# Prompt attention reorganised: three-pass scores on half the array's rows, one transpose bank, TensorE order item by item

## The reference

```python
s = jnp.einsum('bqhmd,bkhmd->bhmqk', qs, ks).astype(F32) * (DIFF_DH ** -0.5)
s = s + bias[None, :, None]
s = jnp.where(rel >= 0, s, jnp.finfo(F32).min)
p = jax.nn.softmax(s, axis=-1)
a = p[:, :, 0] - lam * p[:, :, 1]
return jnp.einsum('bhqk,bkhd->bqhd', a, v.astype(F32))
```

## Time and profile before

| | |
|---|---|
| median of 3 runs | 3955.66 us (3954.72 to 3956.73) |
| the profiled execution | 3956.0 us |
| its span, first to last instruction | 3954.2 us |
| TensorE busy over the span | 92% |
| VectorE, ScalarE, GpSimd busy | 51%, 33%, 8% |
| prompt attention: first DMA to last output tile | 2194.2 to 3076.5 us |

### The profile page before, as it was taken

The page is one execution under the profiler, slowest core; times in us unless marked ns, Lnnn a source line. Parts: engine busy times, 40 slices in busy tenths (PEclk is TensorE's granted clock), DMA queues, the critical chain, the costliest instruction groups (busy, mean ns, idle before and its releaser), DMA issues. The chain is left out here.

```text
span 3954.2 us, 55321 instructions
## 1 busy us (share of the span) xinstructions
PE 3629.8 (92%) x19279; PEld 2987.5 (76%) x19279; DVE 2020.6 (51%) x4394; ACT 1323.2 (33%) x2186; POOL 319.5 (8%) x258
## 2 busy tenths in 40 slices
PE   3999997996999999999999688888898799969999
PEld 3988985774888888888888577777777767558887
DVE  1112111555732642743733588889888222156785
ACT  1112111331221322322322366666666211123332
POOL 0002002111100300200200000000000000022220
PEclk9999997998999999999999899999999899989999
DMA  4323332335334434445443622222210545254541
GB/s 111 98 90 120 102 96 80 112 112 196 115 128 133 165 123 159 160 129 166 147 136 122 134 66 66 55 53 55 66 34 12 205 176 206 106 185 165 170 159 71
DMA packets 364126, 473.00 MB, mean 120 GB/s; under 512 B 157877, under 2 KB 219094, under 8 KB 363878
## 3 DMA queue, kind: packets, MB, share of 16 engines
q1 hardware_dynamic: 363878, 469.77, 37.8%
HBM read 365.20 MB, written 104.47 MB: 119 GB/s over the span
## 5 line engine op out<-in xcount | busy, mean ns | idle before, releaser
L438 PE MATMUL mid_ps_m<-mid_w_hi,mid_x_hi 128*128 128x512 f32 x1632 | 641.0, 393 | 0.5 <-DVE mid_x_lo L594 0.5
L439 PE MATMUL mid_ps_m<-mid_w_lo,mid_x_hi 128*128 128x512 f32 x1632 | 635.8, 390 | 0.0
L440 PE MATMUL mid_ps_m<-mid_w_hi,mid_x_lo 128*128 128x512 f32 x1632 | 635.7, 390 | 0.0
L606 DVE TENSOR_TENSOR mid_w_lo<-mid_stage,mid_w_hi 128x1024 fp32r<-128x1024 f32 x192 | 239.1, 1246 | 234.8 <-ACT mid_w_hi L524 233.4
L438 PE MATMUL in_ps_m<-in_w_hi,in_x_hi 128*128 128x512 f32 (+2 forms) x952 | 344.9, 362 | 12.6 <-DVE in_x_lo L594 12.6
L440 PEld LDWEIGHTS mid_ps_m<-mid_w_hi,mid_x_lo 128*128 128x128 f32 x1632 | 306.7, 188 | 64.3
L438 PEld LDWEIGHTS mid_ps_m<-mid_w_hi,mid_x_hi 128*128 128x128 f32 x1632 | 306.8, 188 | 63.5 <-DVE mid_x_lo L594 1.7
L439 PEld LDWEIGHTS mid_ps_m<-mid_w_lo,mid_x_hi 128*128 128x128 f32 x1632 | 306.9, 188 | 61.4
L440 PE MATMUL in_ps_m<-in_w_hi,in_x_lo 128*128 128x512 f32 (+2 forms) x952 | 343.4, 361 | 0.0
L439 PE MATMUL in_ps_m<-in_w_lo,in_x_hi 128*128 128x512 f32 (+2 forms) x952 | 343.4, 361 | 0.0
L1502 PE MATMUL att_ps_o<-att_v,att_a_t 128*128 128x128 f32 x2176 | 291.8, 282 | 47.0 <-ACT att_a_t L1563 46.1
(11 more groups left out here) (278 smaller groups left out, 5622.0 us busy)
## 6 DMA issues: line engine op xcount, KB each, us to landing
mid_stage<-in_diff_w_in SPq DMA_DIRECT2D x128, 512.0 KB, 3.7
smp_k_pg<-in_cache_k SPq DMA_DIRECT2D x64, 512.0 KB, 5.1
smp_v_pg<-in_cache_v SPq DMA_DIRECT2D x64, 512.0 KB
in_stage<-in_gla_w_in SPq DMA_DIRECT2D x32, 512.0 KB, 4.0
mid_stage<-in_gla_w_out SPq DMA_DIRECT2D x32, 512.0 KB, 5.5
mid_stage<-in_ple_w_gate SPq DMA_DIRECT2D x32, 512.0 KB, 3.5
att_k_nat<-out_k SPq DMA_DIRECT2D x128, 128.0 KB, 2.6
att_q_nat<-diff_q SPq DMA_DIRECT2D x128, 128.0 KB, 2.8
```

The costliest lines, as they stand in the source:

```text
L438: nc.tensor.matmul(dst, x_hi[u][:, k, :], w_hi[r][:, i, 0:W], start=(k == 0), stop=False)
L439: nc.tensor.matmul(dst, x_hi[u][:, k, :], w_lo[r][:, i, 0:W], start=False, stop=False)
L440: mm = nc.tensor.matmul(dst, x_lo[u][:, k, :], w_hi[r][:, i, 0:W], start=False, stop=(k == KD - 1))
L606: nc.vector.tensor_tensor(lo, stage[n % STAGES][:, :, 0:W], hi.bitcast(F32), ALU.subtract).then_inc(s["w_lo_done"], 1)
```

## The change

All 128 items are written out, and each step is made anew. (Lines of the changed kernel are cited as order prints them.)

- Prep: keys and queries come in whole (two DMAs per 512 tokens in place of eight), 8 preps per head. ScalarE copies the transposed bank to `raw`, and GpSimd splits it into `hi` and `lo`.
- Scores: three passes (hi*hi, hi*lo, lo*hi) per m, on the 64 rows of that m, the two m in turn, into two of three slots of 1024 columns. Of a part (up to 1024 keys) all passes are waited for together, and the wait ahead of a part asks for both of its slots.
- Take: one VectorE instruction per part and m with the bias laid out over all keys; one reduce gives the negative maximum. Reciprocal and weight move to GpSimd (three small instructions), the scaled output tile from ScalarE to VectorE.
- Transposes of preps and of `a` share a single bank `ps_a`.
- Queues run at other distances: scores 4 items ahead of the products, take 3, exps 2.

```diff
-        ps_s = [ps(f"ps_s{i}") for i in range(RING)]
-        ps_k = ps("ps_k")
-        ps_a = [ps(f"ps_a{i}") for i in range(2)]
+    LEAD, TAKE, EXP = 4, 3, 2
+    S_BUFS, SLOTS, OUTS = 4, 3, 4
...
+        ps_s = [ps(f"ps_s{i}", WIDE) for i in range(SLOTS)]
+        ps_a = ps("ps_a")
...
+                def scores(n):
...
+                        x = 2 * (first_part[n] + c)
...
+                        if x + 2 > SLOTS:
+                            pe.wait_ge(s["taken"], after(x + 2 - SLOTS))
+                        for a0 in range(first, last, BANK):
+                            a1 = min(a0 + BANK, last)
+                            for step, (left, right) in enumerate(((hi, hi), (hi, lo), (lo, hi))):
+                                for m in range(2):
+                                    rows = slice(m * D_DH, (m + 1) * D_DH)
+                                    mm = nc.tensor.matmul(ps_s[(x + m) % SLOTS][:, a0 - first:a1 - first],
+                                                          left[u][1][rows, i * P:(i + 1) * P],
+                                                          right[u][0][rows, a0:a1], start=(step == 0),
+                                                          stop=(step == 2))
+                            if a1 == last:
+                                mm.then_inc(s["ready"], 1)
...
+                def values(n):
+                    for g in range(turns(n) + 1):
+                        if g < turns(n):
+                            turn(n, g)
+                            yield
+                        if g >= 1:
+                            meet(n, g - 1)
+                            yield
+
+                for n in range(FIRST, N):
+                    for key in preps_at(n):
+                        prep(*key)
+                    for _ in scores(n + LEAD) if 0 <= n + LEAD < N else ():
+                        pass
+                    for _ in values(n) if n >= 0 else ():
+                        pass
...
+                for n in range(FIRST, N):
+                    ahead = 0 <= n + EXP < N
+                    if ahead:
+                        exps(n + EXP, 0)
+                    for key in preps_at(n):
+                        evict(*key)
+                    middle = (turns(n) + 1) // 2 if n >= 0 else 0
+                    copies(n, 0, middle)
+                    if ahead:
+                        exps(n + EXP, 1)
+                    copies(n, middle, turns(n) if n >= 0 else 0)
...
+                for n in range(-TAKE, N + 1):
+                    if n + TAKE < N:
+                        take(n + TAKE)
+                    if 0 <= n < N:
+                        combine(n)
+                    if 1 <= n:
+                        output(n - 1)
```

More of the change, by code:

```diff
@@ L1320, in attention, with at, keys, parts @@
     T = PROMPT_TILES
+    N = D_HEADS * T
     NEAR = 2 * P
[L1322 to L1331, removed]
+    WIDE = 2 * BANK
+    LEAD, TAKE, EXP = 4, 3, 2
+    S_BUFS, SLOTS, OUTS = 4, 3, 4
+    def at(n):
+        return divmod(n, T)
+    def keys(n):
+        return (n % T + 1) * P
+    def parts(n):
+        return [(a, min(a + WIDE, keys(n))) for a in range(0, keys(n), WIDE)]
+    first_part = [sum(len(parts(m)) for m in range(n)) for n in range(N + 1)]
+    def turns(n):
+        return -(-(n % T + 1) // 4)
+    first_turn = [sum(turns(m) for m in range(n)) for n in range(N + 1)]
+    FIRST = -6
+    PREPS = 8
+    def preps_at(n):
+        here = [(0, n - FIRST)] if 0 <= n - FIRST < PREPS else []
+        if 0 <= n < N - T and n % 2 == 0:
+            here.append((n // T + 1, n % T // 2))
+        return here
+    order = [key for n in range(FIRST, N) for key in preps_at(n)]
+    prep_no = {key: m for m, key in enumerate(order)}
+    prep_use, turn_use, uses = {}, {}, 0
+    for n in range(FIRST, N):
+        for key in preps_at(n):
+            prep_use[key] = uses
+            uses += 1
+        for g in range(turns(n) if n >= 0 else 0):
+            turn_use[(n, g)] = uses
+            uses += 1
     with ExitStack() as mem:
@@ L1385, in slots, with evicted_to @@
-        def slots(i):
-            start = sum(beside[:i])
-            return preps[start:start + beside[i]], start
+        v_in = [core.sem(f"att_v_in{u}") for u in range(2)]
+        near_in = [core.sem(f"att_near_in{u}") for u in range(2)]
+        far_in = [core.sem(f"att_far_in{u}") for u in range(2)]
+        stored = [core.sem(f"att_stored{i}") for i in range(OUTS)]
+        def evicted_to(m):
+            return (sum(1 for x in prep_use.values() if x <= m), sum(1 for x in turn_use.values() if x <= m))
@@ L1416, in _ @@
[L1416 to L1438, removed]
@@ L1444, in _, with wait_bank_free @@
+                for i in range(OUTS):
+                    sp.wait_ge(stored[i], after(16 * N // OUTS))
             @block.tensor
             def _(pe):
[L1446 to L1453, removed]
+                def wait_bank_free(m):
+                    if m >= 1:
+                        raws, copies = evicted_to(m - 1)
+                        pe.wait_ge(s["raw_done"], after(raws))
+                        pe.wait_ge(s["a_copied"], after(copies))
@@ L1457, in prep @@
                                                  core.ident[:, :])
                     mm.then_inc(s["turned"], 1)
[L1460 to L1476, removed]
+                def scores(n):
+                    h, i = at(n)
+                    u = h % 2
+                    for c, (first, last) in enumerate(parts(n)):
+                        x = 2 * (first_part[n] + c)
+                        if c == 0:
+                            pe.wait_ge(s["lo_done"], after(prep_no[(h, 2 * (i // 4) + 1)] + 1))
+                        if x + 2 > SLOTS:
[11 more added lines that the diff above has]
+                                mm.then_inc(s["ready"], 1)
@@ L1506, in values @@
[L1506 to L1512 removed]
+                        pe.wait_ge(s["a_done"], after(n + 1))
+                    wait_bank_free(turn_use[(n, g)])
+                    for b in range(4 * g, min(4 * g + 4, n % T + 1)):
+                        mm = nc.tensor.transpose(ps_a[:, (b % 4) * P:(b % 4 + 1) * P], a[n % 2][:, b * P:(b + 1) * P],
+                                                 core.ident[:, :])
@@ L1513, in values @@
+                def values(n):
[3 more added lines that the diff above has]
+                            yield
                         if g >= 1:
+                            meet(n, g - 1)
                             yield
-                def head(H, u, last):
-                    for i in range(T):
-                        todo = [] if last else list(enumerate(slots(i)[0]))
-                        for n, (is_q, m, g) in todo[:1]:
-                            prep(H + 1, slots(i)[1] + n, is_q, m, g)
-                        mixed = values(H, u, i)
-                        if not (last and i + 2 >= T):
-                            ahead_to = ahead(H, u, i, 2)
-                            for step, _ in enumerate(scores(*ahead_to), 1):
-                                if step >= RING and step % 2 == 0:
-                                    next(mixed, None)
-                        for _ in mixed:
-                            pass
-                        for n, (is_q, m, g) in todo[1:]:
-                            prep(H + 1, slots(i)[1] + n, is_q, m, g)
@@ L1666, in head @@
-                def head(H, u, last):
-                    for i in range(T):
-                        if not (last and i + 1 >= T):
-                            take(*ahead(H, u, i, 1))
-                        combine(H, u, i)
-                        if not last:
-                            for n, (is_q, m, g) in enumerate(slots(i)[0]):
-                                low(H + 1, 1 - u, slots(i)[1] + n, is_q, m, g)
-                dve.sem_inc(s["piece_free"], RING)
-                for n, (is_q, m, g) in enumerate(preps):
-                    low(0, 0, n, is_q, m, g, turn_banks)
```

363 lines of the change are left out of this document (178 added, 185 removed).

## The result

The changed kernel takes 4034.01 us (median of 4 runs, 4029.57 to 4036.65) against 3955.19 for the kernel before, measured beside it: ratio 1.0198, 95% interval 1.0186 to 1.021. It is slower by 79 us where 92 were forecast. The profiled execution has a span of 4031.5 us, 77.3 more than the earlier trace rows. Prompt attention's first output tile comes at 2220.2 (8 earlier than in the earlier trace rows) and its last ends at 3152.8 instead of 3076.5, so 76.3 of the 77.3 lie in this stage.

What follows compares the result with a forecast made beforehand. VectorE bounds the kernel before; afterwards TensorE's serial chain does, 118.2 us per head against 107. Start 2218 + 942 for eight heads + 8 contention + 0.4 ends at 3168.4, +92: 4048 us, range 3990 to 4150.

Steps and rivals of the forecast that it cites:

- preps: TensorE's transposes for preps: 8 per head at 0.46 us, four transposes each, 3.7 us per head.
- scores, with restarts: TensorE's score passes: 27.2 us per head, full pieces at 0.69, plus 4.0 for restarting passes after waits.
- slot waits: TensorE waits for VectorE to read map 0 before writing an item's second part: 8 x 1.55 = 12.4 us per head.
- values: TensorE's transposes and products with waits for ScalarE's copies: 68.1 plus 1.6 of restarts, 69.7 us per head.
- waits before an item's first transposes: Late VectorE combinations for items of 2 to 4 blocks, 1.2 us per head.
- Pairs run together: TensorE's 64-row passes of the two maps run concurrently, so a pair costs one pass; full pieces take 0.69 us.
- rival 1: TensorE's paired half-height passes run one after the other: scores 48.8 instead of 27.2 us per head, +173, 4221 us; 9%.
- by fours: Values summed over items of 1-4, 5-8, 9-12 and 13-16 blocks: 6.4, 14.3, 21.5, 25.9 us per head.
- The copy behind the exponential: In a 12-block item, ScalarE's third copy queues behind an exponential of item n+2; TensorE waits about 1 us.
- GpSimd's contention: GpSimd instructions reading SBUF delay VectorE's combinations of small items: 1.0 us per head, 8 in all, bounds 0 and 128.
- rival 2: TensorE's clock falls because its chain idles: 64 items of 5 to 12 blocks lose 1.2 us each, +77, 4125 us; 15%.
- Start: GpSimd's splits and first weights delay prompt attention's chain, which starts in effect at 2218, bounds 2210 and 2226.

## Why the prediction was right

The step that decides held: VectorE is relieved, and the time goes to TensorE's own queue, whose waits nothing fills. The rewrite would have paid without the slot wait (3914) or without the serial order and its companion on VectorE (3898).

Measured from start to start in TensorE's order of time, items at full clock added over a head, us per head:

| term | forecast | measured |
|---|---|---|
| preps | 3.7 | 4.2 |
| scores, with restarts | 31.2 | 29.5 |
| slot waits | 12.4 | 11.8 |
| values | 69.7 | 69.2 |
| waits before an item's first transposes | 1.2 | 0.3 |
| sum | 118.2 | 115.0 |

Heads in fact took 116.1 to 120.7, because the clock was not always granted in full. The last term was forecast for combinations that come late. TensorE's matmuls waited for none: the 0.3 is one wait per head, in the item of 13 blocks, for ScalarE to evict a prep from the single bank.

VectorE and GpSimd in order of time, for the point on contention below:

```profile
2896.02 2.08 DVE L1664 SCALAR_TENSOR_TENSOR att_a<-att_s,att_weight 128x1792 f32<-128x1792 f32 x1
2896.20 3.05 POOL L1596 TENSOR_TENSOR att_k_lo<-att_raw,att_k_hi 128x512 fp32r<-128x512 f32 x1
```

- **Pairs run together:** right, rival 1 is out; the runs with the maps in turn and with the same rows show both why and that, among three passes per map, the order of issue has no part in it. By the Trainium skill, "TensorE: Matmul & The Clock Gate", Part 3, matmuls in different row groups run concurrently, and the trace agrees: 0.23 per pair against 0.47 within one half.
- **Scores:** short pieces were priced at 0.22 per pair, held by weight loads. The trace shows 0.11 for 128 and 256 columns and about 0.18 for 384. With the restarts this term was 1.7 too long.
- **Slots:** 1.47 against 1.55. The run with six slots shows that the wait stood bare: without it and its restarts the stage is 97 us shorter, and 20 more came with the clock.
- **Values:** right by fours (6.4, 14.3, 21.5, 25.9 against 7.2, 14.2, 21.6, 26.2; the forecast's 1.6 of restarts stands beside its fours). The copy behind the exponential was waited for, but less than described: 0.64 in an item of 12 blocks where the prediction looked for about 1. By the forecast's working the exponential cost 61 us, as the expectation of the run that moves it says. The two runs on it show 27 us won back for 5 to 11 blocks, and 33 as the sum for 5 to 12; for 13 and 14 blocks it was not measured by itself. So the near agreement of this term, 69.7 against 69.2, hides an error inside it.
- **GpSimd's contention, 8 us:** nothing on the path. A combination of one size took the same in every head (128x1280: 1552 ns in the mean of eight), except in the first four items and the one of 16 blocks, 2.75 us beside GpSimd's instructions and 2.34 in the last head, which no engine waited for. The two engines do meet, where there is time: GpSimd's `att_k_lo` takes 3.05 us in 7 of 32 cases and 1.27 in the others. In the two rows above it starts inside a combination and ends 1.15 after it.
- **The clock:** priced at nothing in the forecast, 77 in rival 2. It fell where that rival said, in items of 5 to 9 blocks, in which TensorE had just waited 1.47 and 0.78, but for some 20 us: the chain from 2215.7 to the last tile is 936.7, and 8 x 115.0 less the last head's preps is 916. With six slots, without the 1.47, it stayed at 1.00.
- **Start:** 2215.7 in effect instead of 2218.
- **Two readings:** (0.60 - 0.27) / 3 is 0.110, not the 0.116 per transpose that the prediction goes on with; over 168 transposes this is 1.0 per head too much. An 8-row pass takes 0.50 by the earlier trace rows (0.99 for two), not 0.46; that it is no shorter than one over 128 rows stands.

Together, the forecast has 8 x 3.2 too much for the heads and 0.5 for the last one, 8 for GpSimd and 2.3 for the start, and 20.9 too little for the clock: it is 15.6 late at the end of the stage, and so 92 instead of 76. That it came so near is in part luck, since some 36 us too much and 21 too little cancel. The mechanism is not luck: each of its waits was seen and taken away by a run.

## What to carry to other kernels

When work is taken off the engine that is the bound, price the queue that becomes the next one as a chain, wait by wait: a sum of busy times would have said 200 us faster here. Cut a ring of buffers into small pieces where the writer waits for the first reader: the same six banks were worth 120 us more here as six slots than as three. And an order that is changed on one engine needs its counterpart on the others: passes issued among the values gained 12 us alone, and 136 once VectorE combined first.

## What the runs showed of the hardware that was not expected

Passes over the upper and the lower 64 rows run as two streams: three of one half, issued ahead of three of the other, start in step with them, 0.01 us apart (4037.18 us against 4034.01). So the sentence at the start of this text, that each engine takes its queue strictly in order, does not hold for the starts of TensorE's passes over different halves.

In two windows the granted clock was lower although TensorE was busier. With passes that all use one half of the rows it was 0.61 and 0.69 at 87.78 and 86.68 of 100 us busy; with both halves it was 1.00 at 76.85. The two shares are not quite alike, since the same work keeps TensorE busy longer at the lower level, and no run tried the rows and the clock apart.
